# Query and key norms of the mixers: one matmul and a wide reciprocal, or token sums, a narrow root and reciprocal, and a spread

## The reference, cut to what matters

```python
def rmsnorm(x, g):
    xf = x.astype(jnp.float32)
    y = xf * lax.rsqrt(jnp.mean(xf * xf, axis=-1, keepdims=True) + EPS)
    return (y * g.astype(jnp.float32)).astype(x.dtype)
...
        q = rmsnorm(da_q.reshape(B, S, DA_HEADS, 2, DA_QK_DIM), da_q_norm_g[l]) * (DA_QK_DIM ** -0.5)
        k = rmsnorm(da_k.reshape(B, S, DA_HEADS, 2, DA_QK_DIM), da_k_norm_g[l])
        v = da_v.reshape(B, S, DA_HEADS, DA_V_DIM)
        o_da = diff_attention(q, k, v, lam, bias_dist)
```

## Time and profile before

| | us |
|---|---|
| median of 3 runs | 3303.81 |
| lowest and highest | 3298.59, 3304.18 |
| the profiled execution, its own time | 3304.33 |
| its span in the profile | 3302.5 |
| TensorE matmul busy | 3167.6 (96%) |
| VectorE busy | 1832.6 (55%) |
| ScalarE busy | 1161.8 (35%) |
| mean share of TensorE's full clock | 0.982 |

### The profile page before, as it was taken

How to read it: one execution, slowest core, us unless ns; L and a number is a source line. 1 busy time by engine, 2 the same in 40 slices (tenths; PEclk the granted TensorE clock), 3 DMA queues, 4 the chain that set the end, 5 groups by cost and what they waited for, 6 DMA issues and landing times.

```text
span 3302.5 us, 42135 instructions
## 1 busy us (share of the span) xinstructions
PE 3167.6 (96%) x17280; PEld 2505.8 (76%) x17280; DVE 1832.6 (55%) x2842; ACT 1161.8 (35%) x1813; POOL 189.4 (6%) x149
## 2 busy tenths in 40 slices
PE   8999899999999899999899999999999989999999
PEld 6788778887777678887677587788877758778887
DVE  3753453344777754243576745654657674556463
ACT  4533243232433443132453323432335332343232
POOL 1222010001000020001000000000010000010000
PEclk9999999999999989999999999999999999999999
DMA  4210022222112112222211122223231112222322
GB/s 172 81 40 19 8 83 89 102 90 98 64 64 66 63 52 92 100 90 96 92 64 64 52 90 90 94 83 112 76 124 64 64 39 93 97 91 76 110 87 79
DMA packets 41563, 264.88 MB, mean 80 GB/s; under 512 B 4600, under 2 KB 4984, under 8 KB 13980
## 3 DMA queue, kind: packets, MB, share of 16 engines
q1 hardware_dynamic: 41364, 262.18, 23.3%
q10 hardware_dynamic: 8, 0.01, 0.0%
HBM read 260.07 MB, written 3.42 MB: 80 GB/s over the span
## 4 chain that ended last, share of the span: by engine, by line
PE 76%; DVE 9%; ACT 3%; issue 2%; DVEq 0%; ACTq 0%; POOL 0%; POOLq 0%
PE psum L340 22%; PE psum L341 22%; PE psum L342 22%; PE psum L1029 1%; DVE w_lo L321 1%; ACT tiles L1064 1%; PE psum L1038 1%; DVE tiles L1092 1%; PE psum L1997 1%; PE psum L1999 1%; PE psum L1998 1%; PE psum L1909 1%; DVE tiles L1801 1%; DVE tiles L1863 1%; DVE psum L675 1%
## 5 line engine op out<-in xcount | busy, mean ns | idle before, releaser
L340 PE MATMUL psum<-hi,w_hi 128*128 128x512 f32 x3608 | 1448.5, 401 | 19.1 <-DVE w_lo L321 10.0
L341 PE MATMUL psum<-lo,w_hi 128*128 128x512 f32 x3608 | 1429.3, 396 | 0.0
L342 PE MATMUL psum<-hi,w_lo 128*128 128x512 f32 x3608 | 1428.3, 396 | 0.0
L321 DVE TENSOR_TENSOR w_lo<-ring,w_hi 128x1024 fp32r<-128x1024 f32 (+1 forms) x495 | 593.3, 1199 | 427.2 <-ACT w_hi L313 427.1
L340 PEld LDWEIGHTS psum<-hi,w_hi 128*128 128x128 f32 x3608 | 679.7, 188 | 190.3 <-DVE w_lo L321 10.4
L313 ACT ACTIVATE w_hi<-ring 128x1024 fp32r<-128x1024 f32 (+1 forms) x495 | 505.3, 1021 | 887.4 <-PE psum L342 826.9
L341 PEld LDWEIGHTS psum<-lo,w_hi 128*128 128x128 f32 x3608 | 679.5, 188 | 168.7 <-issue 7.0
L342 PEld LDWEIGHTS psum<-hi,w_lo 128*128 128x128 f32 x3608 | 679.0, 188 | 166.6
L772 DVE SCALAR_TENSOR_TENSOR xT<-xT,psum 128x512 f32<-128x512 f32 x96 | 65.9, 687 | 223.3 <-PE psum L342 223.3
L1064 ACT ACTIVATE tiles<-tiles,small 128x256 f32<-128x256 f32 (+3 forms) x176 | 95.0, 541 | 162.1 <-DVE small L1092 161.6
L1677 DVE TENSOR_TENSOR tiles<-tiles 128x512 f32<-128x512 f32 x64 | 44.3, 692 | 174.4 <-ACT tiles L1669 174.4
(11 more groups left out here) (265 smaller groups left out, 2739.1 us busy)
## 6 DMA issues: line engine op xcount, KB each, us to landing
ring<-in_weights SPq DMA_DIRECT2D x211, 1024.0 KB, 4.8
ring<-in_weights SPq DMA_DIRECT2D x28, 704.0 KB, 4.0
ring<-in_weights SPq DMA_DIRECT2D x4, 896.0 KB, 4.5
ring<-in_weights SPq DMA_DIRECT2D x3, 832.0 KB, 4.3
xT<-in_x SPq DMA_DIRECT2D x8, 256.0 KB, 5.9
tiles<-bias_repeated SPq DMA_DIRECT2D x8, 256.0 KB, 6.6
out<-xT SPq DMA_DIRECT2D x8, 256.0 KB, 2.9
held<-in_const SPq DMA_DIRECT2D x1, 1344.0 KB, 8.4
```

Of the source, the lines that this page charges most:

```text
L321: dve.tensor_tensor(self.w_lo[:, n % AHEAD, w], self.raw(n), self.w_hi[:, n % AHEAD, w].bitcast(F32), ALU.subtract).then_inc(self.lo_ready, 1)
L340: pe.matmul(out, hi, rhs.hi(first + at), start=(at == 0), stop=False)
L341: pe.matmul(out, hi, rhs.lo(first + at), start=False, stop=False)
L342: last = pe.matmul(out, lo, rhs.hi(first + at), start=False, stop=(at == end))
```

## The change

The norm of a tile becomes two steps in two ticks, 16 ticks in all, at projection ticks u + 1. In step 0 (odd projection ticks) ScalarE squares the tile; TensorE sums by tokens into 128x8 of bank 3; ScalarE takes the root of these 128x8 values into `values`, columns 56 to 63 of the small tile; VectorE takes their reciprocal. In step 1 (even ticks) TensorE spreads the values over bank 3, and VectorE multiplies tile, gain and the bank. The root now stands in the tick of its own sum, and the sum of norm n waits until the gains of norm n - 1 have read the bank.

```diff
-    squared, mean_done, root, inverse, cleared, masked, normed, lam_sum, lam_exp, chain = (k.sem() for _ in range(10))
+    squared, sums_done, root, inverse, spread_done, cleared, masked, normed, lam_sum, lam_exp, chain = (k.sem() for _ in range(11))
     src = [k.tile(4 * (n % 2) + n // 2) for n in range(8)]
-    lam = k.small[:, 40:44]
+    lam, values = k.small[:, 40:44], k.small[:, 56:64]
...
-    def scalar(act, n):
-        if n >= 1:
-            act.wait_ge(mean_done, n)
-            act.activation(sq[(n - 1) % 2], k.bank(bank), ACT.Sqrt, bias=k.eps(64e-6 if n % 2 else 1e-6)).then_inc(root, 1)
-        if n < 8:
+    def scalar(act, t):
+        n, step = t // 2, t % 2
+        if step == 0:
             act.wait_ge(copied, 3 * (n // 2) + n % 2 + 1)
             if n >= 2:
-                act.wait_ge(normed, n - 1)
+                act.wait_ge(sums_done, n - 1)
             act.activation(sq[n % 2], src[n], ACT.Square).then_inc(squared, 1)
-        if n == 1:
+            if n >= 1:
+                act.wait_ge(spread_done, n)
+            act.wait_ge(sums_done, n + 1)
+            act.activation(values, k.bank(bank)[:, 0:2 * TB], ACT.Sqrt, bias=k.eps(1e-6 if n % 2 else 64e-6)).then_inc(root, 1)
+        if t == 1:
             act.wait_ge(lam_sum, 2)
             act.activation(lam[:, 0:2], lam[:, 0:2], ACT.Exp).then_inc(lam_exp, 1)
 
-    def tensor(pe, n):
-        if n < 8:
+    def tensor(pe, t):
+        n, step = t // 2, t % 2
+        if step == 0:
             pe.wait_ge(squared, n + 1)
             if n >= 1:
-                pe.wait_ge(root, n)
-            pe.matmul(k.bank(bank), k.c("mean64" if n % 2 else "sum64"), sq[n % 2], start=True, stop=True).then_inc(mean_done, 1)
+                pe.wait_ge(normed, n)
+            token_sums(pe, k.bank(bank), sq[n % 2], k.c("mean64" if n % 2 else "sum64")[:, 0:P:64]).then_inc(sums_done, 1)
+        else:
+            pe.wait_ge(inverse, n + 1)
+            spread_tokens(k, pe, k.bank(bank), values, 2).then_inc(spread_done, 1)
 
-    def vector(dve, n):
-        if n == 0:
+    def vector(dve, t):
+        n, step = t // 2, t % 2
+        if t == 0:
...
-        if n >= 1:
-            m, rs = n - 1, sq[(n - 1) % 2]
-            dve.wait_ge(root, n)
-            dve.reciprocal(rs, rs).then_inc(inverse, 1)
-            dve.wait_ge(inverse, n)
-            if m % 2 == 0:
-                dve.scalar_tensor_tensor(out=src[m], in0=src[m], scalar=k.v("da_q_g", l), in1=rs,
+        if step == 0:
+            dve.wait_ge(root, n + 1)
+            dve.reciprocal(values, values).then_inc(inverse, 1)
+        else:
+            rs = k.bank(bank)
+            dve.wait_ge(spread_done, n + 1)
+            if n % 2 == 0:
+                dve.scalar_tensor_tensor(out=src[n], in0=src[n], scalar=k.v("da_q_g", l), in1=rs,
                                          op0=ALU.mult, op1=ALU.mult).then_inc(normed, 1)
...
-        if n == 2:
+        if t == 3:
...
-    w = Work(9, tensor, scalar, vector, gpsimd)
+    w = Work(16, tensor, scalar, vector, gpsimd)
...
-    stage(k, begin + behind(proj, [(heads, lambda u: 3 * (u // 2) + u % 2 + 1), (second, lambda u: 12),
+    stage(k, begin + behind(proj, [(heads, lambda u: u + 1), (second, lambda u: 12),
```

More of the change, by code:

```diff
@@ L1807, in vector @@
                 up = slice(64, 128)
-                ch(dve.scalar_tensor_tensor(out=k.tile(26 + m // 2)[up], in0=src[m][up], scalar=k.v("da_k_g", l)[up],
+                ch(dve.scalar_tensor_tensor(out=k.tile(26 + n // 2)[up], in0=src[n][up], scalar=k.v("da_k_g", l)[up],
                                             in1=rs[up], op0=ALU.mult, op1=ALU.mult))
-                ch.then(dve.scalar_tensor_tensor(out=src[m][0:64], in0=src[m][0:64], scalar=k.v("da_k_g", l)[0:64],
+                ch.then(dve.scalar_tensor_tensor(out=src[n][0:64], in0=src[n][0:64], scalar=k.v("da_k_g", l)[0:64],
                                                  in1=rs[0:64], op0=ALU.mult, op1=ALU.mult))
-                dve.memset(src[m][up], 0.0).then_inc(normed, 1)
-        if n == 2:
+                dve.memset(src[n][up], 0.0).then_inc(normed, 1)
+        if t == 3:
             dve.wait_ge(lam_exp, 1)
```

## The result

The changed kernel takes 3315.47 us in the median of six runs (3314.16 to 3316.86); the kernel before takes 3303.77 in six beside them. The ratio of the two is 1.0037, with a 95% interval of 1.0027 to 1.0047: slower by 11.7 us. The forecast was 3307.7 with a range up to 3313. The profiled execution took 3314.16 (span 3312.3), 9.8 more than the one of before.

What follows compares the result with a forecast made beforehand. TensorE, on 76% of the chain, was taken as the bound, with VectorE sometimes late. 20.0 - 13.6 - 6.2 + 3.7 - 0.5 = +3.4 us on 3304.33 gave 3307.7 us, range 3299 to 3313.

Steps and rivals of the forecast that it cites:

- Part 1: TensorE's added work: sum and spread in place of one matmul, 1.25 us a norm, +20.0 us for 16 norms.
- The rival of cheap norms: TensorE's pieces cost only their weight loads, 0.8 us a norm; 3296.8 us in all, chance 0.12.
- Part 2: TensorE's waits for the square and copy L1079 go, -13.6 us, and the slow clock behind the long ones, -6.2 us.
- All six waits: TensorE's idle times of 0.84, 3.11, 2.88 in layer 0 and 0.83, 3.11, 2.87 in layer 1: -13.6 us.
- Part 3: The new order of norm steps in 16 ticks makes TensorE wait 1.85 us a layer, +3.7 us.
- The other term, 1.7 in tick 12: With a key, VectorE's gains, clearing and copy L1079 outlast transposes and scores: TensorE waits 1.7 us.
- The 0.15 of tick 10: With a query, VectorE's gain and copy take 1.2 us against 1.05 of scores: TensorE waits 0.15 us.
- The -0.5 at the stage's start: Layer 0's first norm: the sum replaces a matmul run at half clock; half of 1 us counted, -0.5 us.
- 6.2 us for the falls that go: Slow clock behind the 3.11 and 2.88 us waits disappears, 1.5 and 1.6 us lost there, -6.2 us for two layers.
- a separate rival: The clock falls behind the 2.73 and tick 12 waits of both layers, 4 x 1.6 us: 3314.1 us, chance 0.14.
- The rival of waits that stay: Waits move instead of going, VectorE reaches L1079 as late as before: +20, 3324 us, chance 0.06.
- The signs read beforehand: Over layer 0's norms TensorE's idle falls some 5 us, busy rises some 8; one 1.7 us wait at tick 12, clock 1.00.

Runs made afterwards that it cites:

- e6: The changed kernel with the root's table loaded early and VectorE's part of the norms issued behind attention's in each tick: 3306.65 us, ratio 1.0015.
- e4: The kernel before without its 16 wide reciprocals, tiles multiplied by the root, so the division is left out: 3284.45 us, ratio 0.9942.
- e1: The changed kernel with a one-column root that loads the root's table before ScalarE waits for the sum: 3311.46 us, ratio 1.0024.
- e2: The changed kernel with root and small reciprocal one tick later, in the even tick ahead of the spread: 3316.58 us, ratio 1.0048.
- e8: The kernel before with only VectorE's part of the norms moved behind attention's in each tick: 3324.58 us, ratio 1.0054.
- e5: The kernel before with ScalarE's logarithm and exponential in place of root and wide reciprocal: 3298.12 us, ratio 0.9987.
- e9: e5 with ScalarE's square placed ahead of the logarithm in its tick: 3300.58 us, ratio 0.9995.
- e3: The changed kernel with a second, redundant spread ahead of each spread: 3327.73 us, ratio 1.0098.
- e12: e9 with VectorE's rotations moved behind attention's part of their tick: 3291.93 us, ratio 0.9968 to the kernel before.

## Why the prediction was wrong

The sum had 3.4 us, and the norms' stretch alone cost 7.5 (two layers); in the profiled executions falls of the clock elsewhere cost another 4.5, in the medians 4.2 are left for them. The 4.1 between 3.4 and 7.5 are, from the ladder doubled: the pieces -0.7, the old lateness -1.5, the new lateness +5.7, the stage's start +0.5. By the prediction's own steps:

**Part 1 held.** Forecast 1.25 us a norm; the rows of after give 2.11 for sum and spread, and e6 against e4 gives 1.21, 19.3 us in all against 20.0. By the Trainium skill's rule on weight loads (TensorE: Matmul & The Clock Gate, section LDWEIGHTS) the estimate was 13.6; the measurement decides for the rows of this kernel's first block. The rival of cheap norms is out.

**Part 2 held in place and was a little small.** All six waits went. With their slow stretches they were worth 10.64 a layer by e4, where the prediction had 6.8 + 3.1 = 9.9.

**Part 3 failed, at the edit costed at nothing: "the activation tables are swapped as often as before, six times to the root and seven to the exponential a layer, by following the order".** The count was right (12 loads at L1776). What counts is where a load stands. Before, the sum that the root waits for came from an earlier tick; now it is of the same tick, and all 12 loads start only when TensorE has done it, so 1.28 us of load moved onto the path sum, root, reciprocal, copy. The prediction had "in an odd tick root, small reciprocal and copy are short beside the transposes and scores that TensorE issues meanwhile: no wait". Against 1.46 us of scores (L1029) they are short only without the load. Measured: 0.61 + 1.24 = 1.85 idle a layer, 3.7 us; e1 gives back 3.5 to 4.0 in the median and 2.3 a layer in the trace. The other term, 1.7 in tick 12, measured 1.57. The 0.15 of tick 10 is there too, as 0.28, though no row has it in brackets: in the changed kernel L1038 starts 0.72 behind the scores,

```profile
1691.32 0.61 PE L1029 MATMUL psum<-tiles 128*128 128x128 f32 x4
1692.04 0.91 PE L1038 MATMUL psum<-tiles 128*128 128x128 f32 x6
```

and in e6 0.44 (1693.64 to 1694.08). In tick 9 the load costs 0.24 in the same hidden way (1681.62 to 1683.58 is 1.96, in e6 1.72), and in e1 this is gone while tick 10's stays. Together the new lateness cost 4.72 a layer against 1.85 forecast, more than the 3.42 of idle time in brackets: 0.5 are these two, and the rest some 0.25 beyond the row of each of the three waits.

**The -0.5 at the stage's start was not there.** From the first sum to the first spread are 8.81 us; from the first norm to the second were 8.83.

**The clock was the second failure, in size and in weight.** The sum took 6.2 us for the falls that go, and a separate rival, with a chance of 0.14, held that they come back elsewhere; its 3314.1 is where the result lies. That number was met in part by luck. It was made of four falls, behind the 2.73 waits of both layers and the 1.7 of tick 12 in both, and only one of the four came; the table load, which it did not have, filled much of the rest. The trace has new falls behind the 2.73 of layer 0 only (+1.55), behind the 2.52 of layer 0 (+1.63) and behind a 2.08 at 2891 (+1.5), and a clock of 1.00 around tick 12. The prediction's step was "these idle times are too short to cost clock: behind 2.73 us at 1777.07 it stays at 1.00"; behind the same wait of the changed kernel it did not. The sum counted as a property of two waits what comes and goes between executions. How much falls elsewhere cost a version, as the distance of its median from the kernel before less twice what its layer 0 took longer (one profiled execution each, so rough): 4.2 for the changed kernel, 6.1 for e2, 5.4 for e1, 5.2 for e6, 4.3 for e8, 4.7 for e5, 6.6 for e9, 2.5 for e4 and 0.2 for e3. So some 4 us came with nearly every change of this stretch, with or without token sums; why the kernel before has so few is not settled. The mean clock says it more simply: 0.982 in the profiled executions of both kernels, although two long waits a layer were gone. That the six runs of after all have these falls is argued from their mean clocks (0.980 to 0.983), not shown.

The rival of waits that stay is out. The signs read beforehand came out mixed: over the 153 and 157 us TensorE's idle time fell by 3.2 (10.5 to 7.3) and its busy time rose by 6.9, where 5 and 8 were forecast.

## What to carry to other kernels

When a step of ScalarE is moved next to the one that it waits for, look in the trace where its table load stands: here it came behind the wait, and one tiny activation of the same function ahead of the wait let it run while the engine waited anyway. To take work off an engine that is late but not the bound, also try moving it in the order or to a third engine. Here the order alone lost 21 us (e8), a third engine won 5 (e5, not clear of no change), and that with the square first and the rotations moved 11.7 (e12); putting it on the engine that bounds cost its full price, 1.2 us for each of 16 norms against some 1.3 us of lateness. And where the clock falls behind waits, a saving that a single trace shows is uncertain by what comes back elsewhere, here some 4 us.

## What the runs showed of the hardware that was not expected

- The clock at its lower level stayed there through up to 38 us of uninterrupted matmuls, most with half the rows or columns (a stretch of 34.9 us became 46.1 in five places and 52.4 in two). In other executions it was back after some 3 us in the same stretch (36.3 to 36.5), as behind full products.
- Waits of the same length from the same cause fell in one kernel and not in the other: 2.73 at 1777 against 1779, 2.52 at 1817 against 1820, 2.08 at 2883 against 2891. In the kernel before the 2.52 of layer 0 had no fall behind it and that of layer 1 had one. Beside their place in time, nothing that tells them apart was found.
- Where a table load stands to a wait differs within one kernel. All 12 loads of the root (L1776, ahead of which the program has two waits) start when TensorE's sum is done. A load for the exponential (L1064, one wait) runs ahead of the wait, in the changed kernel in tick 12:

```profile
1707.08 1.28 ACT L1064 ACT_TABLE_LOAD   x1
1709.41 0.51 ACT L1064 ACTIVATE tiles<-tiles,small 128x256 f32<-128x256 f32 x1 [1.05 <-DVE small L1092]
```

  What decides this no run tested; whether the root's load would have run early with one wait less stays open.
- An activation with a new function starts 1.30 us after its table load does (1716.78 to 1718.08), and the load at 1737.12 follows directly on a copy that starts at 1736.51 and takes 0.59: the load and nothing more. The Trainium skill (ScalarE: Activation LUTs, section What ACT_TABLE_LOAD costs) has the same 1283 ns, and a drain of about 1380 ns besides, with which these rows disagree. Its section Table sets says that logarithm and exponential in a row need one load since a set holds both; in e5 a load stands ahead of each, two a norm.
